# Feed-forward gate and up products as a 2x2 block product of seven parts, with tokens in two spans

## The chip, the cores and the metric

The program runs on one core of one Trainium2 chip, in one launch. The metric is the device time of that core in microseconds (us), as the median of several runs.

## The reference

One inference step of a decoder layer, for 1024 prompt tokens and 8 x 4 = 32 sample tokens, 1056 together, with a model width of 1024, all in float32:

```
x  = x + 0.5 * ffn1(rmsnorm(x, n_ffn1))
x  = x + mixer(rmsnorm(x, n_mix))          # attention and pooling, not touched by the change
x  = x + 0.5 * ffn2(rmsnorm(x, n_ffn2))
y  = rmsnorm(x, n_final)
ffn(h) = (silu(h @ w_gate) * (h @ w_up)) @ w_down     # w_gate, w_up: 1024 x 2816, w_down: 2816 x 1024
rmsnorm(x, g) = x * rsqrt(mean(x * x) + 1e-6) * g
```

## The kernel before

The residual `xT` lies transposed in SBUF, with the 1024 features as 8 tiles of 128 partitions and the 1056 tokens along the free dimension, in three chunks of 352 (`CH`). Every product of two float32 matrices is made of three matmuls: each operand is split into a high part, which is the value rounded to the type fp32r, and a low part, the value less its high part, and `product3` (lines 112 to 114) adds hi x hi, hi x lo and lo x hi into one PSUM bank.

`stage_ffn` is called twice. The 2816 hidden features are 22 tiles (`FT`), taken in 11 pairs by a loop on each engine; the first and the last pair are written out. For each tile the gate and up weights (2 x 8 x 128 x 128) are loaded into `gu_raw`, copied to `gu_hi` by ScalarE (line 458) and their low parts subtracted by VectorE (line 541). TensorE then makes, for each of three chunks, 24 matmuls of 352 columns for gate and 24 for up. VectorE multiplies gate by the tokens' inverse root (`norm.inv`, line 572), ScalarE takes Silu (line 464), VectorE multiplies by the inverse root again (574) and by up (578), and splits the result into `a_hi` (581) and `a_lo` (583). After two tiles the down product follows: 24 blocks (3 chunks x 8 feature tiles) of 6 matmuls, each added to `xT` by one VectorE operation (line 589). The down weights are split like the others (lines 481 and 609).

RMSNorm is late: the products take x times gain (`in_h_hi` and `in_h_lo`, in the second stage `f_h_hi` and `f_h_lo`, lines 157 and 195), and the inverse root, which is made meanwhile (lines 201 to 215), is applied behind the product. For the second feed-forward, chunks 0 and 1 of these halves and the inverse roots are made in the last part of `stage_out_project`. In the first, the next stage's halves are made in the last pair. At the end of the second, `FinishRows` turns the result into rows of 128 tokens on TensorE (line 269), normalizes them and stores them; rows 0 to 4 are turned within the last pair, the others behind it.

GpSimd has no arithmetic in the feed-forward loops. Its subtracts that rows below show belong to the compression stage (cs), where it shares the making of low parts with VectorE (lines 1041 and 1035 on GpSimd, 1160, 1176 to 1178 and 1184 on VectorE).

## Time and profile before

| | us |
|---|---|
| median of three runs | 2868.22 (2865.53 to 2868.45) |
| span of the profiled execution | 2868.9 |
| TensorE busy with matmuls | 2649.2 (92%) |
| VectorE busy | 1484.9 (52%) |
| ScalarE busy | 885.1 (31%) |
| GpSimd busy | 384.7 (13%) |
| mean granted clock of TensorE | 0.975 of full speed |

Busy time is the time in which an instruction of an engine ran; matmuls overlap, so the distance between the starts of two of them says how long each takes of the stream. The granted clock is a share of 2.4 GHz. The profiled execution lies 0.7 us above the median.

### The profile page before, as it was taken

What the parts mean: (1) busy time and instruction counts of PE and PEld (TensorE: products, weight loads), DVE (VectorE), ACT (ScalarE), POOL (GpSimd) and SP (SyncE); (2) the same over time, 40 slices, a digit from 0 to 9 for tenths busy, and PEclk for the clock granted to TensorE, in tenths of its full rate; (3) what the DMA queues carried; (4) which work ended last, traced back from release to release, by engine and by line L of the source; (5) the groups of instructions that cost most, each with busy time, mean ns of one, the idle gap of its engine ahead of it and who ended that gap; (6) DMA issues with size and microseconds to landing.
All of it is one profiled execution on the core that took longest, in us unless ns stands there. A gap on an engine that the chain in (4) does not pass through costs nothing. (4 is left out here: it accounts for less than half of the span.)

```text
span 2868.9 us, 44901 instructions
## 1 busy us (share of the span) xinstructions
PE 2649.2 (92%) x17616; PEld 2498.9 (87%) x17616; DVE 1484.9 (52%) x2887; ACT 885.1 (31%) x1570; POOL 384.7 (13%) x427
## 2 busy tenths in 40 slices
PE   4999998999999999999978888777999999999997
PEld 4888887999999999988966666556999999999997
DVE  5444445554444444464147768555464444444445
ACT  4656655111111111032246656444221111111112
POOL 4444441000000000000012222452000000000001
PEclk9999999999999999999979979899999999999999
DMA  4131313211111110021311010586031111111101
GB/s 180 64 125 64 125 56 119 74 46 58 55 47 44 44 44 29 15 100 43 101 62 45 24 44 34 185 279 226 16 88 45 45 55 46 44 44 44 51 15 61
DMA packets 171831, 206.88 MB, mean 72 GB/s; under 512 B 15342, under 2 KB 153455, under 8 KB 169002
## 3 DMA queue, kind: packets, MB, share of 16 engines
q1 hardware_dynamic: 161026, 144.91, 16.3%
q0 software_dynamic: 10672, 60.19, 5.7%
q8 instruction: 86, 1.41, 0.2%
q14 instruction: 47, 0.39, 0.0%
HBM read 191.39 MB, written 18.01 MB: 73 GB/s over the span
## 5 line engine op out<-in xcount | busy, mean ns | idle before, releaser
L464 ACT ACTIVATE f_act_gate<-f_act_gate 128x352 f32<-128x352 f32 x132 | 65.8, 498 | 1185.3 <-DVE f_act_gate L572 1185.2
L589 DVE SCALAR_TENSOR_TENSOR trunk<-f_down,trunk 128x352 f32<-128x352 f32 x528 | 275.9, 524 | 205.3 <-PE f_down L114 205.3
L112 PE MATMUL f_down<-f_a_hi,f_wd_hi 128*128 128x352 f32 x1056 | 341.1, 323 | 0.0
L114 PE MATMUL f_down<-f_a_hi,f_wd_lo 128*128 128x352 f32 x1056 | 340.3, 322 | 0.0
L113 PE MATMUL f_down<-f_a_lo,f_wd_hi 128*128 128x352 f32 x1056 | 339.3, 321 | 0.0
L112 PE MATMUL cs_sum<-cs_x_hi,cs_w_hi 128*128 128x256 f32 (+1 forms) x768 | 230.3, 300 | 33.0 <-DVE cs_x_lo L1184 21.6
L114 PE MATMUL cs_sum<-cs_x_hi,cs_w_lo 128*128 128x256 f32 (+1 forms) x768 | 218.0, 284 | 0.0
L113 PE MATMUL cs_sum<-cs_x_lo,cs_w_hi 128*128 128x256 f32 (+1 forms) x768 | 217.6, 283 | 0.0
L1041 POOL TENSOR_TENSOR cs_x_lo<-cs_x,cs_x_hi 128x516 fp32r<-128x516 f32 x128 | 170.9, 1335 | 235.4 <-ACT cs_x_hi L1098 235.4
L114 PEld LDWEIGHTS f_down<-f_a_hi,f_wd_lo 128*128 128x128 f32 x1056 | 199.1, 189 | 0.0
L113 PEld LDWEIGHTS f_down<-f_a_lo,f_wd_hi 128*128 128x128 f32 x1056 | 198.7, 188 | 0.1
L112 PEld LDWEIGHTS f_down<-f_a_hi,f_wd_hi 128*128 128x128 f32 x1056 | 198.1, 188 | 0.1
L578 DVE TENSOR_TENSOR f_act_up<-f_act_gate,f_up 128x352 f32<-128x352 f32 x132 | 68.8, 521 | 244.2 <-PE f_up L114 243.9
L112 PEld LDWEIGHTS cs_sum<-cs_x_hi,cs_w_hi 128*128 128x128 f32 x768 | 146.5, 191 | 44.1 <-DVE cs_x_lo L1184 41.9
L572 DVE TENSOR_TENSOR f_act_gate<-f_gate,f_inv 128x352 f32<-128x352 f32 x132 | 69.0, 523 | 214.5 <-PE f_gate L114 214.2
L112 PE MATMUL f_gate<-f_h_hi,f_gu_hi 128*128 128x352 f32 x528 | 170.1, 322 | 3.2 <-DVE f_gu_lo L557 3.2
L112 PE MATMUL f_gate<-in_h_hi,f_gu_hi 128*128 128x352 f32 x528 | 171.4, 325 | 0.0
L113 PE MATMUL f_gate<-in_h_lo,f_gu_hi 128*128 128x352 f32 x528 | 171.0, 324 | 0.0
L114 PE MATMUL f_gate<-in_h_hi,f_gu_lo 128*128 128x352 f32 x528 | 170.9, 324 | 0.0
L114 PE MATMUL f_up<-f_h_hi,f_gu_lo 128*128 128x352 f32 x528 | 170.5, 323 | 0.0
L114 PE MATMUL f_gate<-f_h_hi,f_gu_lo 128*128 128x352 f32 x528 | 170.5, 323 | 0.0
L113 PE MATMUL f_gate<-f_h_lo,f_gu_hi 128*128 128x352 f32 x528 | 170.3, 323 | 0.0
(421 smaller groups left out, 6745.6 us busy)
## 6 DMA issues: line engine op xcount, KB each, us to landing
f_gu_raw<-in_w_ffn_gate_dram SPq DMA_DIRECT2D x44, 512.0 KB, 4.3
f_gu_raw<-in_w_ffn_up_dram SPq DMA_DIRECT2D x44, 512.0 KB, 5.7
as_pages<-in_cache_kv_slc_dram SPq DMA_DIRECT2D x128, 128.0 KB, 4.0
as_pages<-in_cache_kv_slc_dram POOLq DMA_DIRECT2D x128, 128.0 KB, 4.0
at_spread<-saved_rows SPq DMA_DIRECT2D x16, 768.0 KB, 3.9
in_w_raw<-in_w_ffn_down_dram SPq DMA_DIRECT2D x11, 1024.0 KB, 5.0
f_wd_raw<-in_w_ffn_down_dram SPq DMA_DIRECT2D x11, 1024.0 KB, 5.0
x_saved<-trunk SPq DMA_DIRECT2D x2, 2112.0 KB, 14.8
```

Source lines behind the costliest of these rows:

```text
L112: pe.matmul(out, w_hi, x_hi, start=first, stop=False)
L113: pe.matmul(out, w_hi, x_lo, start=False, stop=False)
L114: return pe.matmul(out, w_lo, x_hi, start=False, stop=last)
L464: act.activation(act_gate[:, b, :], act_gate[:, b, :], ACT.Silu).then_inc(silu_done, 1)
L572: dve.tensor_tensor(act_gate[:, b, :], gate_bank[b][:, 0:CH], inv, ALU.mult).then_inc(gate_scaled, 1)
L578: dve.tensor_tensor(act_up[:], act_gate[:, b, :], up_bank[b][:, 0:CH], ALU.mult).then_inc(pair_free, 1)
L589: dve.scalar_tensor_tensor(xT[:, m, chunk(c)], down_bank[n % 4][:, 0:CH], 0.5, xT[:, m, chunk(c)], ALU.mult, ALU.add).then_inc(down_free, 1)
L1041: pool.tensor_tensor(x_lo[s][:, 0:ODD], x[s][:, 0:ODD], x_hi[s][:, 0:ODD].bitcast(F32), ALU.subtract).then_inc(diff_lo_done, 1)
```

## The change

Gate and up of one tile, over 2 x 264 tokens, are a 2x2 block product: the weights' halves (gate and up, each with features 0 to 511 and 512 to 1023) times the tokens' halves (features 0 to 511 and 512 to 1023, each for 264 tokens `near` and 264 tokens `far`). Eight block products and four additions become seven block products (Winograd's form), four sums of weight blocks (`w_sum`), four differences of token blocks (`b_sum`), and additions of the results. Each block product is 4 x 3 matmuls of 264 columns (`HT`).

- The tokens are taken in two spans of 528: all 22 tiles for the first span, then all 22, backwards, for the second. A step `g` is one tile for one span; 44 steps, in 22 pairs `q`, with a down product of 16 blocks of 6 matmuls behind each pair. The weights are loaded twice, but for the tile at which the order turns.
- GpSimd makes the four weight sums of the next tile, the low parts of two of the seven weight blocks (4 and 6) and one addition of results (`up_far`) in each step. VectorE makes the low parts of the other five, the other additions (`base`, `above`, `far`, `up_near`), and as before the multiplications, the splits and the updates. ScalarE makes the high parts and copies two products out of PSUM, whose banks are then added onto.
- Weight blocks have one buffer each: the high part of block i of the next tile is written when product i of this step is done.
- The inverse root is now multiplied into the operands, so that it is needed before the first product; operands are made once for each span, at the start and during pair 10, by VectorE (`scaled`, `difference`, `low_b`), ScalarE and GpSimd (`last_b`, `low_b`). `stage_out_project` no longer makes halves for the second feed-forward.
- In the second feed-forward rows 0 to 3 are finished in pairs 16 to 19 (`EARLY`), rows 4 and 5 are turned in the last pair, the others behind it.
- All loops over pairs are written out. The split token operands `b_hi` and `b_lo` lie in the buffers of the halves before; a new `b_sum` of 8 x 4 x 264 floats for each partition is added.

The core of the diff, without empty lines, and with less indentation:

```diff
+    STEPS, PAIRS, WEIGHTS = 2 * FT, FT, 2 * FT - 1
+    KH = KT // 2
+    ON_DVE, ON_POOL = (0, 1, 2, 3, 5), (4, 6)
+    SUM_OF = {1: 0, 2: 1, 3: 2, 5: 3}
+    PLACED = (0, 2, 3, 1, 0, 2, 3)
...
+    def sums(v):
+        raw = gu_raw[v % 2]
+        gate_1, gate_2, up_1, up_2 = raw[:, 0, 0:KH], raw[:, 0, KH:KT], raw[:, 1, 0:KH], raw[:, 1, KH:KT]
+        pool.wait_ge(raw_landed[v % 2], 32 * (v // 2) + 32)
+        if v:
+            pool.wait_ge(w_lo_dve, 5 * (v - 1) + 2)
+        pool.tensor_tensor(w_sum[:, 0], up_1, up_2, ALU.add).then_inc(w_summed, 1)
+        if v:
+            pool.wait_ge(w_lo_dve, 5 * (v - 1) + 3)
+        pool.tensor_tensor(w_sum[:, 1], gate_1, up_1, ALU.subtract).then_inc(w_summed, 1)
+        if v:
+            pool.wait_ge(w_lo_dve, 5 * (v - 1) + 4)
+        pool.wait_ge(w_summed, 4 * v + 1)
+        pool.tensor_tensor(w_sum[:, 2], w_sum[:, 0], gate_1, ALU.subtract).then_inc(w_summed, 1)
+    def last_sum(v):
+        if v:
+            pool.wait_ge(w_lo_dve, 5 * (v - 1) + 5)
+        pool.wait_ge(w_summed, 4 * v + 3)
+        pool.tensor_tensor(w_sum[:, 3], gu_raw[v % 2][:, 0, KH:KT], w_sum[:, 2],
+                           ALU.subtract).then_inc(w_summed, 1)
+    def low_w(v, i):
+        pool.wait_ge(w_hi_done, 7 * v + i + 1)
+        pool.tensor_tensor(w_lo[:, i], form(v, i), w_hi[:, i].bitcast(F32), ALU.subtract).then_inc(w_lo_pool, 1)
+    def last_b(span):
...
+        if span:
+            pool.wait_ge(product_done, 7 * FT)
+        pool.tensor_tensor(b_sum[:, 6], b_sum[:, 4], b_sum[:, 3], ALU.subtract).then_inc(b_last_made, 1)
+    def low_b(span, i):
+        pool.wait_ge(b_hi_done, 7 * span + {5: 4, 6: 7}[i])
+        pool.tensor_tensor(b_lo[:, i], b_sum[:, i], b_hi[:, i].bitcast(F32), ALU.subtract).then_inc(b_lo_pool, 1)
+    def operands(span):
+        last_b(span)
+        low_b(span, 5)
+        low_b(span, 6)
...
+    for g in range(STEPS):
+        v = next_weights(g)
+        pool.wait_ge(above_done, g + 1)
+        pool.wait_ge(fifth_copied, g + 1)
+        if g:
+            pool.wait_ge(far_done, g)
+        pool.tensor_tensor(up_far[:], above[:], fifth_copy[:], ALU.add).then_inc(up_far_done, 1)
+        if v is not None:
+            low_w(v, 4)
+            if v + 1 < WEIGHTS:
+                sums(v + 1)
+            low_w(v, 6)
+            if v + 1 < WEIGHTS:
+                last_sum(v + 1)
...
+    def high_w(v, i):
+        if i in SUM_OF:
+            act.wait_ge(w_summed, 4 * v + SUM_OF[i] + 1)
+        else:
+            act.wait_ge(raw_landed[v % 2], 32 * (v // 2) + 32)
+        if v:
+            before = v - 1 if v <= FT - 1 else v
+            act.wait_ge(product_done, 7 * before + i + 1)
+        act.activation(w_hi[:, i], form(v, i), ACT.Copy).then_inc(w_hi_done, 1)
...
+    def copy_out(g, target, bank, nth, copied_sem, free_sem):
+        act.wait_ge(product_done, 7 * g + nth + 1)
+        if g:
+            act.wait_ge(free_sem, g)
+        act.activation(target[:], bank_set[g % 2][bank][:, 0:HT], ACT.Copy).then_inc(copied_sem, 1)
...
+    for q in range(PAIRS):
+        fresh = q == 0 or down_of(q) != down_of(q - 1)
+        for g in (2 * q, 2 * q + 1):
+            v = next_weights(g)
+            copy_out(g, first_copy, 0, 0, first_copied, base_done)
+            if v is not None:
+                high_w(v, 0)
+            copy_out(g, fifth_copy, 2, 1, fifth_copied, up_far_done)
+            if v is not None:
...
+                norm.square(act, xT, 2)
+            if fresh and g == 2 * q and q:
+                high_down(down_of(q), 0)
+            if v is not None:
+                high_w(v, 2)
+                high_w(v, 3)
+            if fresh and g == 2 * q and q:
+                high_down(down_of(q), 1)
+            act.wait_ge(product_done, 7 * g + 5)
+            if g:
+                act.wait_ge(a_near, g)
+            act.activation(near[:], bank_set[g % 2][0][:, 0:HT], ACT.Silu).then_inc(silu_near, 1)
+            if v is not None:
+                high_w(v, 4)
+            if g == 1:
+                act.wait_ge(norm.sum_done, 6)
+                for s in range(2):
+                    high_down(0, s)
...
+            if g == 1:
                 norm.root(act, 2)
-        act.wait_ge(wd_landed, 16 * i + 16)
-        act.wait_ge(down_done, DOWNS * i + ONE)
-        act.activation(wd_hi[:], wd_raw[:], ACT.Copy).then_inc(wd_hi_done, 1)
-        if not last:
...
+    def scaled(span, k0, first, step):
+        part = slice(2 * span * HT, 2 * span * HT + 2 * HT)
+        for k in range(KH):
+            made = dve.scalar_tensor_tensor(
+                b_sum[:, first:first + step + 1:step, k, :],
+                xT[:, k0 + k, part].rearrange("p (h n) -> p h n", h=2), norm.gain[:, k0 + k:k0 + k + 1],
+                inv[:, part].rearrange("p (h n) -> p h n", h=2), ALU.mult, ALU.mult)
+        made.then_inc(b_made, 1)
...
+    def difference(out, a, b):
+        dve.tensor_tensor(b_sum[:, out], b_sum[:, a], b_sum[:, b], ALU.subtract).then_inc(b_made, 1)
+    def low_b(span, i):
+        dve.wait_ge(b_hi_done, 7 * span + {0: 1, 1: 2, 4: 3, 2: 5, 3: 6}[i])
+        dve.tensor_tensor(b_lo[:, i], b_sum[:, i], b_hi[:, i].bitcast(F32), ALU.subtract).then_inc(b_lo_dve, 1)
...
+    def left_operands(span):
+        if span:
+            dve.wait_ge(product_done, 7 * (FT - 1) + 1)
+        scaled(span, 0, 0, 7)
+        dve.wait_ge(b_made, 5 * span + 1)
...
+        dve.wait_ge(b_made, 5 * span + 2)
+        low_b(span, 0)
+    def right_operands(span):
+        if span:
+            dve.wait_ge(product_done, 7 * (FT - 1) + 6)
+        scaled(span, KH, 4, 1)
+        dve.wait_ge(b_made, 5 * span + 3)
+    def middle_operands(span):
+        difference(2, 5, 7)
+        difference(3, 5, 1)
+        dve.wait_ge(b_made, 5 * span + 5)
...
+    def multiply(g, h, gate, up, gate_ready, up_ready, done, hi_done, ready):
+        s = tile_of(g) % 2
+        dve.wait_ge(gate_ready, g + 1)
+        dve.wait_ge(up_ready, g + 1)
+        dve.tensor_tensor(gate[:], gate[:], up[:], ALU.mult).then_inc(done, 1)
+        dve.wait_ge(done, g + 1)
+        dve.tensor_copy(a_hi[:, s, h], gate[:]).then_inc(hi_done, 1)
+        dve.wait_ge(hi_done, g + 1)
+        dve.tensor_tensor(a_lo[:, s, h], gate[:], a_hi[:, s, h].bitcast(F32), ALU.subtract).then_inc(ready, 1)
...
+    def update(q, n):
+        h, m = order_of(q)[n // KT], n % KT
+        span = 0 if q < FT // 2 else 1
+        dve.wait_ge(down_done, DOWNS * q + n + 1)
+        dve.scalar_tensor_tensor(xT[:, m, half_of(span, h)], bank_set[0][n % 4][:, 0:HT], 0.5,
+                                 xT[:, m, half_of(span, h)], ALU.mult, ALU.add).then_inc(down_free, 1)
...
+    for q in range(PAIRS):
+        fresh = q == 0 or down_of(q) != down_of(q - 1)
+        for g in (2 * q, 2 * q + 1):
+            v = next_weights(g)
+            banks = bank_set[g % 2]
+            if v is not None:
+                low_w(v, 0)
+                low_w(v, 1)
...
+            if fresh and g == 2 * q and q:
+                low_down(down_of(q), 0)
+            if v is not None:
+                low_w(v, 2)
+            dve.wait_ge(product_done, 7 * g + 4)
+            dve.wait_ge(first_copied, g + 1)
+            if g:
+                dve.wait_ge(up_near_done, g)
+            dve.tensor_tensor(base[:], first_copy[:], banks[1][:, 0:HT], ALU.add).then_inc(base_done, 1)
+            dve.wait_ge(base_done, g + 1)
+            if g:
+                dve.wait_ge(up_far_done, g)
+            dve.tensor_tensor(above[:], base[:], banks[3][:, 0:HT], ALU.add).then_inc(above_done, 1)
+            if v is not None:
+                low_w(v, 3)
+            if fresh and g == 2 * q and q:
+                low_down(down_of(q), 1)
+            dve.wait_ge(product_done, 7 * g + 6)
+            if g:
+                dve.wait_ge(a_far, g)
+            dve.tensor_tensor(far[:], base[:], banks[2][:, 0:HT], ALU.add).then_inc(gate_far_done, 1)
+            if g == 1:
+                for s in range(2):
+                    low_down(0, s)
+            multiply(g, 1, far, up_far, silu_far, up_far_done, far_done, a_hi_far, a_far)
...
+            dve.tensor_tensor(up_near[:], base[:], banks[3][:, 0:HT], ALU.add).then_inc(up_near_done, 1)
+            multiply(g, 0, near, up_near, silu_near, up_near_done, near_done, a_hi_near, a_near)
+            if v is not None:
+                low_w(v, 5)
+            if g == 0:
+                norm.fold(dve, 2)
+            if g == 1:
...
+    def product(g, i):
+        span, first, in_set = g // FT, g % FT == 0, g % 2
+        v = weights_of(g)
+        if i in ON_DVE:
+            pe.wait_ge(w_lo_dve, 5 * v + ON_DVE.index(i) + 1)
+        else:
+            pe.wait_ge(w_lo_pool, 2 * v + ON_POOL.index(i) + 1)
+        if first and i < 5:
+            pe.wait_ge(b_lo_dve, 5 * span + i + 1)
+        elif first:
+            pe.wait_ge(b_lo_pool, 2 * span + i - 4)
+        if i < 4 and in_set == 0 and g:
+            pe.wait_ge(down_free, DOWNS * (g // 2 - 1) + 13 + PLACED[i])
...
+        elif i < 4 and g > 1:
+            pe.wait_ge((silu_near, base_done, gate_far_done, up_near_done)[PLACED[i]], g - 1)
+        elif i >= 4:
+            pe.wait_ge({4: first_copied, 5: fifth_copied, 6: above_done}[i], g + 1)
+        if finish and in_set and i == 0 and g // 2 - 1 in EARLY:
+            fin.wait_taken(pe, EARLY[g // 2 - 1])
...
+            mm = product3(pe, out, w_hi[:, i, k, :], w_lo[:, i, k, :], b_hi[:, i, k, :], b_lo[:, i, k, :],
+                          k == 0 and i < 4, k == KH - 1, i >= 4)
+        mm.then_inc(product_done, 1)
...
+    def down_part(q, n, part):
+        h, m = order_of(q)[n // KT], n % KT
+        s = tile_of(2 * q + part) % 2
+        if n % KT < 4:
+            pe.wait_ge((a_near, a_far)[h], 2 * q + part + 1)
+        if part == 0:
+            if n >= 4:
+                pe.wait_ge(down_free, DOWNS * q + n - 3)
+            else:
+                pe.wait_ge((silu_near, base_done, gate_far_done, up_near_done)[n], 2 * q + 1)
+        return product3(pe, bank_set[0][n % 4][:, 0:HT], wd_hi[:, s, m * P:(m + 1) * P],
+                        wd_lo[:, s, m * P:(m + 1) * P], a_hi[:, s, h], a_lo[:, s, h], part == 0, part == 1)
...
+    for q in range(PAIRS):
+        for g in (2 * q, 2 * q + 1):
+            for i in range(7):
+                product(g, i)
...
+                    norm.total(pe, bank_set[0][3], 2)
+        pe.wait_ge(wd_split, down_of(q) + 1)
+        if q == 0:
+            pe.wait_ge(norm.var_done, CHUNKS)
+        for n in range(4):
+            down_part(q, n, 0)
+        for n in range(4):
+            down_part(q, n, 1).then_inc(down_done, 1)
+        for n in range(4, DOWNS):
+            down_part(q, n, 0)
...
-        norm.high(act, xT, mix_hi, c)
...
-        dve.wait_ge(done, KT)
-        norm.low(dve, xT, mix_hi, mix_lo, 0, range(m, m + 1))
...
-        if m < 4:
-            dve.wait_ge(done, 2 * KT)
-            norm.low(dve, xT, mix_hi, mix_lo, 1, range(2 * m, 2 * m + 2))
```

The form of a block is a piece of `gu_raw` for 0, 4 and 6, and of `w_sum` for 1, 2, 3 and 5. Behind both steps of a pair VectorE runs the 16 updates, in the order n = 0 to 15.

## Rows read from the trace of the kernel before

**Rows 1.** Busy time of the engines in stretches, granted clock (PEclk), DMA share, GB/s.

```profile
core 0: us, PE busy (x) PEld busy (x) DVE busy (x) ACT busy (x) POOL busy (x), PEclk, DMA share, GB/s
471.60:1231.00 759.40, 755.71 (x4712) 754.95 (x4712) 389.89 (x660) 113.69 (x130) 4.55 (x9) 1.00 0.16 49
2080.00:2849.00 769.00, 766.59 (x4796) 765.40 (x4796) 384.55 (x664) 111.89 (x128) 3.85 (x3) 1.00 0.16 46
1640.00:1710.00 70.00, 55.40 (x280) 41.63 (x280) 43.48 (x95) 36.95 (x119) 21.72 (x25) 0.78 0.12 46
```

**Rows 2.** TensorE's waits in the two feed-forward stretches: total, times, longest.

```profile
PE f_down L181 <- DVE f_sq L172: 3.7, 1, 3.7
...
PE f_gate L112 <- DVE f_gu_lo L557: 3.2, 1, 3.2
```

**Rows 3.** Matmuls in order of time (start, length), first and last of 18 and 15.

```profile
1227.75 0.32 PE L112 MATMUL f_down<-f_a_hi,f_wd_hi 128*128 128x352 f32 x1
...
1230.47 0.32 PE L114 MATMUL f_down<-f_a_hi,f_wd_lo 128*128 128x352 f32 x1
...
394.14 0.28 PE L112 MATMUL cs_sum<-cs_x_hi,cs_w_hi 128*128 128x256 f32 x1
...
395.80 0.28 PE L114 MATMUL cs_sum<-cs_x_hi,cs_w_lo 128*128 128x256 f32 x1
```

**Rows 4.** VectorE (DVE) and GpSimd (POOL) in order of time, compression stage.

```profile
32.46 0.68 DVE L1160 TENSOR_TENSOR cs_w_lo<-cs_w_whole,cs_w_hi 128x512 fp32r<-128x512 f32 x1
...
33.17 1.74 POOL L1041 TENSOR_TENSOR cs_x_lo<-cs_x,cs_x_hi 128x516 fp32r<-128x516 f32 x1 [1.64 <-ACT cs_x_hi L1098]
...
33.67 1.79 DVE L1160 TENSOR_TENSOR cs_w_lo<-cs_w_whole,cs_w_hi 128x512 fp32r<-128x512 f32 x1
...
34.87 1.73 POOL L1035 TENSOR_TENSOR cs_w_whole<-cs_w_whole 128x512 f32<-128x512 f32 x1
35.38 1.25 DVE L1176 COPY cs_x<-cs_pe 128x2 f32<-128x2 f32 x1
```

**Rows 5.** Groups of VectorE: line, names, shapes, count, busy us, mean ns, idle before.

```profile
L581 DVE CAST f_a_hi<-f_act_up 128x352 fp32r<-128x352 f32 x132 | 45.4, 344 | 4.5
...
L169 DVE TENSOR_TENSOR f_sq<-f_sq 128x1408 f32<-128x1408 f32 x2 | 3.2, 1617 | 0.0
...
L172 DVE TENSOR_TENSOR op_w_raw<-op_w_raw 128x704 f32<-128x704 f32 x2 | 1.8, 892 | 0.1
```

**Rows 6.** The same view for ScalarE (ACT).

```profile
L1091 ACT ACTIVATE cs_x<-cs_turn 128x256 f32<-128x256 f32 x128 | 48.0, 375 | 35.9 <-PE cs_turn L1273 35.9
...
L1070 ACT ACTIVATE cs_w_hi<-cs_w_whole 128x512 fp32r<-128x512 f32 x12 | 6.6, 616 | 0.0
...
L468 ACT ACTIVATE f_gu_hi<-f_gu_raw 128x1024 fp32r<-128x1024 f32 x2 | 2.0, 1048 | 11.0 <-PEq L2745 11.0
```

**Rows 7.** The same view for GpSimd.

```profile
L1885 POOL TENSOR_TENSOR trunk<-at_scaled,at_upper 64x256 f32<-64x256 f32 x32 | 23.1, 723 | 2.5
...
L1880 POOL TENSOR_TENSOR at_scaled<-at_scaled 128x512 f32<-128x512 f32 x16 | 20.4, 1272 | 20.9 <-DVE at_scaled L2004 20.6
```

**Rows 8.** Again VectorE and GpSimd in order of time, compression stage.

```profile
335.02 1.31 POOL L1041 TENSOR_TENSOR cs_x_lo<-cs_x,cs_x_hi 128x516 fp32r<-128x516 f32 x1 [2.52 <-ACT cs_x_hi L1098]
...
335.34 0.42 DVE L1177 TENSOR_TENSOR cs_x<-cs_turn,cs_x 128x256 f32<-128x256 f32 x1 [0.96 <-ACT cs_x L1091]
...
336.01 0.60 DVE L1184 TENSOR_TENSOR cs_x_lo<-cs_x,cs_x_hi 128x256 fp32r<-128x256 f32 x1
```

**Rows 9.** Loads: destination and source, count, KB each, median us to landing.

```profile
f_gu_raw<-in_w_ffn_up_dram SPq DMA_DIRECT2D x44, 512.0 KB, 5.7
```

**Rows 10.** VectorE in order of time at the start of the first feed-forward.

```profile
466.08 0.52 DVE L201 TENSOR_SCALAR f_var<-f_down 128x352 f32<-128x352 f32 x1 [2.06 <-PE f_down L187]
...
475.62 2.34 DVE L207 RECIPROCAL f_inv<-f_inv 128x352 f32<-128x352 f32 x1
```

**Rows 11.** Gate matmuls of both stages: ns min/median/max, first and last start in us.

```profile
L112 PE MATMUL f_gate<-in_h_hi,f_gu_hi x528: 320/323/807, 471.6 to 1211.0; 128*128 128x352 f32 x176
...
L112 PE MATMUL f_gate<-f_h_hi,f_gu_hi x528: 318/323/592, 2080.4 to 2815.8; 128*128 128x352 f32 x176
```

More of the change, by code:

```diff
@@ new lines, in stage_ffn @@
+        a_lo = mem.sb(scope, name + "_a_lo", [P, 2, 2, HT], F32R)
+        first_copy, fifth_copy, base, above, up_far, up_near, far, near = [
+            mem.sb(scope, f"{name}_{part}", [P, HT])
+            for part in ("first", "fifth", "base", "above", "up_far", "up_near", "far", "near")]
+        doubles = [mem.ps(scope, f"{name}_bank{i}", (P, 2 * BANK)) for i in range(4)]
+        singles = [x[:, i * BANK:(i + 1) * BANK] for x in doubles for i in range(2)]
+        bank_set = [singles[0:4], singles[4:8]]
@@ new lines, in high_down @@
+                def high_down(w, s):
+                    act.wait_ge(wd_landed, 16 * w + 16)
+                    q = w if w < FT // 2 else w + 1
+                    if q:
+                        act.wait_ge(down_done, DOWNS * q)
+                    act.activation(wd_hi[:, s], wd_raw[:, s], ACT.Copy).then_inc(wd_hi_done, 1)
+                for c in range(0 if prepared else 2):
+                    norm.square(act, xT, c)
+                if not prepared:
+                    norm.root(act, 0)
```

596 lines of the change are left out of this document (289 added, 307 removed).

## The prediction

> **What bounds the kernel now.** I read the busy tenths first: TensorE is at 9 in every slice of the two feed-forward stages (about 471 to 1231 us, and 2080 to 2849 us), then the stretches themselves [rows 1]. There TensorE is busy 755.7 of 759.4 us and 766.6 of 769.0 us at the full granted clock (1.00, its 2.4 GHz level), VectorE about half, ScalarE a seventh, GpSimd almost not at all. The lists of waits have 3.7 us for TensorE at the beginning of the first and 3.2 at the beginning of the second as their largest rows [rows 2]. So both stages are a gapless stream of matmuls, and their length is count times slot. Slots come from starts in order of time [rows 3]: 18 matmuls of 352 columns start from 1227.75 to 1230.47, so 2.72/17 = 0.160 us each; 15 of 256 columns start from 394.14 to 395.80, 1.66/14 = 0.1185. One feed-forward is 3168 gate and up matmuls (22 tiles x 3 chunks x 2 x 8 x 3) and 1584 down matmuls, 4752 x 0.1597 = 759 us, which the stretch confirms.
>
> **TensorE after the change.** A product is 4 x 3 matmuls of 264 columns. Between the two measured sizes a slot is 0.1185 + (8/96) x 0.0415 = 0.122. One step (one tile, one span) is 84 matmuls, 10.2 us; two steps and their down part (96 matmuls, 11.7 us), a pair, are 264 x 0.1215 = 32.1 us, and a feed-forward has 22 pairs. The old kernel takes 759/22 = 34.5 us for the same work. TensorE alone would win 2.4 us a pair, 44 x 2.4 = 106 us in all. The question is what the other engines do to the 32.1.
>
> **Their new work, per step.** VectorE: five low halves of 512 elements (0.68 long, next start 0.60 later [rows 4]), four adds of a PSUM bank, twice multiply, cast, subtract. An element costs it 1.03 ns (1408 against 704 elements: (1617 - 892)/704 [rows 5]), so a 264-element operation is 0.43 to 0.44 (892 - 440 x 1.03 ns); a cast is 0.34 at 352 [rows 5], about 0.28 here. In the even step of a pair come two low halves of the down weights, 1024 elements, 1.22 each by the same rate. After the steps come 16 updates of 0.43. Sum for a pair: 10 x 0.68 + 8 adds and 8 multiply/subtracts x 0.43 + 4 casts x 0.28 + 2 x 1.22 + 16 x 0.43 = 24.1 us. ScalarE: seven copies of 512 (0.62), two of 264 (0.38), two Silu (taken as 0.42), and in the even step 2 x 1.05 [rows 6]: 6 to 8 us of a 10.2 us step. GpSimd, idle before: six operations of 512 at 1.27 and one of 264 (0.74, between 0.72 at 256 and 1.27 at 512) [rows 7]: 8.4 us a step, 16.7 a pair.
>
> No engine has more than 32.1 us of work. If that were all, the only gap would be before the fifth down block, 0.6 us, since VectorE comes to its updates 0.6 us late: a pair of 32.8.
>
> **The row that decides.** Rows 4 show VectorE and GpSimd together. VectorE starts three subtracts of two SBUF inputs, of 0.68 us alone; GpSimd's subtract is issued at 33.17, under the second. It lasts to 34.91 (1.74 rather than 1.27: it began when the second VectorE operation ended). VectorE's third, issued at 33.67, lasts 1.79: it ended 0.55 after GpSimd's. GpSimd's next, issued at 34.87, lasts 1.73, and under it a two-element copy of VectorE takes 1.25. One operation of each, in turn, and each waits for the whole of the other. At 335 to 337 us [rows 8] two VectorE operations with one input in PSUM run at 0.41 to 0.42 under a GpSimd operation, and the third, with both inputs in SBUF, takes 0.60 and ends 0.28 after it. So what collides is: two SBUF inputs or an SBUF to SBUF copy on VectorE, against GpSimd's two-input operations.
>
> This is a rule of the Trainium skill, SBUF — State Buffer, section Who interferes with whom: VectorE and GpSimd share one port pair that is locked for a whole instruction, and a VectorE instruction with two SBUF inputs, or a copy in a 2-port mode, contends with a GpSimd instruction that reads SBUF. The trace agrees, 1.79 against 0.68 us. By this rule a pair comes to 42.0 below; without it, to 32.8.
>
> In the new loops a pair holds this resource 16.7 us for GpSimd and, on VectorE, for 10 low halves, 2 down halves, 8 multiply/subtracts and 4 casts, some 11 to 14 us: 28 to 31 of 32.1. That alone would just fit. But both engines run in written order, and VectorE's order is a chain that TensorE waits for.
>
> **Walk through a pair** (us from TensorE's first product; a product's result is visible 0.2 after its slots). Even step: VectorE is alone until *above* is made at 7.85, because GpSimd's loop begins by waiting for *above*; product 6, due at 8.76, needs it and starts in time. From then on both have work. GpSimd: up_far to 9.1, low 4 10.2 to 11.45, three sums and low 6 to 17.6. VectorE: second down half 9.1 to 10.2, far add 10.6, Silu on ScalarE to 11.1, and then multiply, cast, subtract, multiply, cast each behind one GpSimd operation: the step ends with low 5 at 18.9, where it would be 13.9 alone. Odd step (TensorE from 10.2): product 5 needs that low 5 and starts at 19.1, not 17.5 (1.6 late). Then low 0, GpSimd's last sum (1.25), low 1, low 2, base, above: 22.75; product 6 starts at 22.9 and ends at 24.4, where the even flow would be 20.4 (another 2.3 to 2.4). The first four down halves end at 25.9; the rest needs a_far: low 3, far add, Silu 24.25, multiply behind low 4 (25.65), cast behind sum 0 (27.1), subtract behind sum 1: 28.65. TensorE waits 2.9. Next, near multiply and cast, behind sum 2 and low 6, its subtract, and low 5 end at 32.65, and only then come the updates: the fifth down block, ready at 30.2, starts at 33.2, 3.0 late. Twelve blocks of 0.73 later the pair ends at 42.0. Stalls 1.6 + 2.3 + 2.9 + 3.0 = 9.8. Nothing is carried over: at 42.6 VectorE and GpSimd are drained, so the next pair is the same. Raw weights are not late: the load waits for low 6 (17.6), lands 5.7 us later [rows 9], and the sum that reads it starts at 25.6.
>
> Bounds of a pair: 37 if half of the blocked operations slip through between GpSimd's, 45 if semaphore steps cost 0.1 more at each of some 30 links. I take the walk, as every link in it has a row: 42.0. Feed-forward loops: 44 x (42.0 - 34.5) = **+330**.
>
> **Beginnings.** Stage one now needs both inverse roots before a product. On VectorE: mean square (466.6 [rows 10]), low 0 (470.5), invert 4.5 (reciprocal 2.34 and four small ones, 0.52 like the mean square or less [rows 10]), mean square, five lows, invert again: 482.5; four scalings of 528 elements (2.8), difference and low of 1056 (1.2 each): product 0 at 487.8. Right operands 2.8, middle 2.4, four lows of 1.2, with three 2.4 us operations of GpSimd in turn between them: the first step ends at 509, as if it had begun at 499. Before, the first gate matmul was at 471.6 [rows 11] with 3.7 us of wait behind it: **+24** (16 without collisions). Stage two has its roots, but the same operands to make: scaling from 2078, last product near 2110, as if begun at 2100, against 2080.4 [rows 11] and 3.2 of wait [rows 2]: +16, less 3 for the halves no longer made in the output projection, whose TensorE hardly waited for them: **+13**. The change of span in pair 10 adds VectorE 5.2 us before base, 2.8 before the updates, 7 among them, and 7 on GpSimd, less one step without weights: 8 each, **+16**. The last rows: four go early, about 2 us of VectorE each, and five turns leave the last pair, **+2** (from -5 to +8). Moved waits on SP's queue: its loads have slack, 0. Unrolled loops: 0, as cs matmuls that are written out one by one keep 0.1185 [rows 3].
>
> The granted clock falls to 0.78 in a stretch where TensorE is fed in pieces [rows 1]; a pair's 17 us of pieces at that level would cost 7.3/0.78 - 7.3 = 2.1, most of it under waits. I take 0 and keep 44 x 2 = 88 as the far end.
>
> Sum: 330 + 24 + 13 + 16 + 2 = 385. The profiled span is 2868.9, 0.7 over the median of the runs, so 2868.2 + 385 = **3253 us**, own range 3160 to 3350.
>
> **Rivals.**
> *Half the collisions* (0.18): GpSimd and VectorE fall into a phase in which the short casts and adds slip past. Pair 37.5: 44 x 3.0 + 45 = 3045. For it: VectorE's holds are shorter than its durations (0.55 of 0.68). Against: rows 4 and 8 show no operation that slipped.
> *TensorE still bounds* (0.10), the other side: the waits are covered, pair 32.8, 44 x -1.7 = -75, beginnings and seam without collisions 16 + 8 + 10 + 2: 2829. It decides from the point where a pair stays under 34.5 - 36/44 = 33.7, that is where collisions cost TensorE less than 0.9 a pair. For it: no engine is over its 32.1. Against it: five blocked operations in the even step alone.
> *Slow clock as well* (0.10): pieces of 1.5 us with gaps of 2 to 3 us hold TensorE at its 1.2 GHz level past the stall, pair 44 to 45: 3253 + 88 to 130, about 3360.
> *The forecast* (0.60). The rest (0.02): about no change.
>
> **Numbers.** Predicted 3253. The range must reach towards the half-collision case and the clock case: 3020 to 3350 leaves out the TensorE case, most of the clock case and little else. 0.2% (6 us) is what a measurement can tell. Faster 0.10, same 0.02, slower 0.88.
>
> **What would show it.** Right: TensorE busy about 0.75 to 0.8 in the new loops, waits of matmuls on a_lo, above, w_lo and trunk of 2 to 3 us each per pair; low halves of 512 on VectorE with a mean well above 0.68 and some at 1.8; GpSimd 512 operations above 1.27; slots of 0.122; first product near 488. Wrong: TensorE at 0.98 and VectorE subtracts at 0.68 while GpSimd works, or stalls that sit on loads or on ScalarE. The prediction fails if GpSimd's operations fall in time where VectorE does updates, which have a PSUM input.

## The result, and the profile after

| | before | after |
|---|---|---|
| median, us | 2867.93 (2865.53 to 2868.45) | 3208.74 (3204.67 to 3215.08, four runs) |
| span of the profiled execution | 2868.9 | 3209.6 |
| mean granted clock | 0.975 | 0.936 |

The ratio is 1.1189, 95% interval [1.1167, 1.1212]: 341 us slower, where 385 were forecast; 3208.7 lies inside the range of 3020 to 3350.

By stretches of the two traces: the first feed-forward, from 471.6 us to the end of its last update (1241.2 before, 1420.8 after), grew from 769.6 to 949.2 (+179.6). What lies between the two became 3.6 shorter. The second, from the last update of the output projection to its own last update, grew from 773.0 to 941.7 (+168.8), and the end became 4.0 shorter. Together that is +341, the difference of the two spans.

The page of the kernel after: busy time of the engines, then their tenths in 40 slices, which for TensorE (PE) were 9 in these stages before.

```profile
PE 2666.7 (83%) x19728; PEld 2478.3 (77%) x19728; DVE 2192.5 (68%) x3746; ACT 1258.6 (39%) x2397; POOL 1280.2 (40%) x1043
...
PE   5999976888888888889988888779588888888887
```

Stretches, with columns as in [rows 1]: the whole first stage, the whole second, one pair of 40.2 us, 3 us behind a stall in it, and eight pairs in a row.

```profile
471.60:1420.80 949.20, 778.28 (x5816) 755.66 (x5816) 754.09 (x1113) 305.57 (x556) 447.70 (x313) 0.92 0.25 74
2253.30:3195.30 942.00, 779.05 (x5860) 757.64 (x5860) 754.19 (x1120) 317.02 (x569) 452.93 (x313) 0.93 0.25 74
703.00:743.20 40.20, 34.35 (x264) 33.44 (x264) 32.34 (x49) 12.71 (x24) 19.94 (x15) 0.96 0.28 79
706.00:709.00 3.00, 2.11 (x10) 1.80 (x9) 2.93 (x5) 0.00 (x0) 1.70 (x3) 0.60 0.02 6
603.90:931.26 327.36, 278.61 (x2114) 271.32 (x2113) 258.45 (x385) 101.71 (x193) 159.21 (x113) 0.94 0.27 78
```

VectorE (DVE) is busy less than TensorE in the pair, and TensorE 34.35 of 40.2 us, so neither is full. [Rows 1] had 755.71 of 759.40. What TensorE waits for, as in [rows 2]:

```profile
PE f_bank L113 <- DVE f_above L806: 93.7, 42, 5.5
PE f_bank L113 <- DVE f_a_lo L756: 80.1, 40, 2.2
PE f_bank L113 <- DVE trunk L762: 70.1, 48, 2.4
...
PE f_bank L113 <- DVE f_w_lo L689: 31.4, 39, 13.1
```

In every pair these are three waits of 1 to 2 us, on `above`, on `a_lo` and on the updates (`trunk`), and a short one on a low part of the weights. All are waits for VectorE; none of a size is for loads or ScalarE. VectorE's odd step in order of time (start, length), as in [rows 4]:

```profile
699.17 0.43 DVE L806 TENSOR_TENSOR f_above<-f_base,f_bank 128x264 f32<-128x264 f32 x1
...
701.03 1.32 DVE L752 TENSOR_TENSOR f_far<-f_far,f_up_far 128x264 f32<-128x264 f32 x1 [0.49 <-ACT f_far L643]
702.38 1.25 DVE L754 CAST f_a_hi<-f_far 128x264 fp32r<-128x264 f32 x1
703.67 1.37 DVE L756 TENSOR_TENSOR f_a_lo<-f_far,f_a_hi 128x264 fp32r<-128x264 f32 x1
704.97 0.42 DVE L822 TENSOR_TENSOR f_up_near<-f_base,f_bank 128x264 f32<-128x264 f32 x1
705.49 0.98 DVE L752 TENSOR_TENSOR f_near<-f_near,f_up_near 128x264 f32<-128x264 f32 x1
706.50 1.26 DVE L754 CAST f_a_hi<-f_near 128x264 fp32r<-128x264 f32 x1
707.80 0.43 DVE L756 TENSOR_TENSOR f_a_lo<-f_near,f_a_hi 128x264 fp32r<-128x264 f32 x1
708.15 0.68 DVE L689 TENSOR_TENSOR f_w_lo<-f_w_sum,f_w_hi 128x512 fp32r<-128x512 f32 x1
708.75 1.95 DVE L762 SCALAR_TENSOR_TENSOR trunk<-f_bank,trunk 128x264 f32<-128x264 f32 x5
```

GpSimd in the same 9 us:

```profile
699.67 1.14 POOL L502 TENSOR_TENSOR f_up_far<-f_above,f_fifth 128x264 f32<-128x264 f32 x1 [2.03 <-DVE f_above L806]
700.77 1.29 POOL L472 TENSOR_TENSOR f_w_lo<-f_gu_raw,f_w_hi 128x512 fp32r<-128x512 f32 x1
702.02 1.46 POOL L454 TENSOR_TENSOR f_w_sum<-f_gu_raw 128x512 f32<-128x512 f32 x1
703.44 1.31 POOL L457 TENSOR_TENSOR f_w_sum<-f_gu_raw 128x512 f32<-128x512 f32 x1
704.72 1.46 POOL L461 TENSOR_TENSOR f_w_sum<-f_w_sum,f_gu_raw 128x512 f32<-128x512 f32 x1
706.14 1.47 POOL L472 TENSOR_TENSOR f_w_lo<-f_gu_raw,f_w_hi 128x512 fp32r<-128x512 f32 x1
```

And TensorE's waits in this step, the matmul that ended each and, in brackets, its length and who ended it:

```profile
699.74 0.36 PE L113 MATMUL f_bank<-in_h_hi,f_w_hi 128*128 128x264 f32 x1 [2.06 <-DVE f_above L806]
705.10 0.59 PE L113 MATMUL f_bank<-f_a_hi,f_wd_hi 128*128 128x264 f32 x1 [2.21 <-DVE f_a_lo L756]
709.23 0.39 PE L113 MATMUL f_bank<-f_a_hi,f_wd_hi 128*128 128x264 f32 x1 [1.12 <-DVE trunk L762]
```

From these rows: the ends of VectorE's multiply (702.35), cast (703.63) and subtract (705.04) lie 0.29, 0.15 and 0.29 us behind the end of a GpSimd operation (702.06, 703.48, 704.75). The addition at 704.97, with an input in PSUM, takes its 0.42. From 707.61 on GpSimd has nothing to do, and the next subtract takes 0.43. Three groups by line over both stages follow, with their means. Undisturbed, this subtract takes 0.43 us, the cast 0.30 and GpSimd's addition 0.74:

```profile
L756 DVE TENSOR_TENSOR f_a_lo<-f_far,f_a_hi 128x264 fp32r<-128x264 f32 x88 | 114.8, 1305 | 3.0
...
L754 DVE CAST f_a_hi<-f_far 128x264 fp32r<-128x264 f32 x88 | 103.6, 1177 | 3.0
...
L502 POOL TENSOR_TENSOR f_up_far<-f_above,f_fifth 128x264 f32<-128x264 f32 x88 | 98.5, 1119 | 718.6 <-DVE f_above L806 718.6
```

### The profile page after: what moved, and what is told of

The parts are those of the page before. It is cut to its first block and busy times, and to the rows that moved or that the text cites. A ratio compares the mean times of both kernels' runs of the same rounds, so it can differ in the third digit from the quotient of the medians.

```text
span 3209.6 us, 52342 instructions
## 1 busy us (share of the span) xinstructions
PE 2666.7 (83%) x19728; PEld 2478.3 (77%) x19728; DVE 2192.5 (68%) x3746; ACT 1258.6 (39%) x2397; POOL 1280.2 (40%) x1043
## 5 line engine op out<-in xcount | busy, mean ns | idle before, releaser
L113 PE MATMUL f_bank<-f_a_hi,f_wd_hi 128*128 128x264 f32 x1408 | 444.3, 316 | 159.1 <-DVE f_a_lo L756 80.1
L114 PE MATMUL f_bank<-f_a_lo,f_wd_hi 128*128 128x264 f32 x1408 | 432.8, 307 | 0.0
L115 PE MATMUL f_bank<-f_a_hi,f_wd_lo 128*128 128x264 f32 x1408 | 432.1, 307 | 0.0
L113 PE MATMUL f_bank<-in_h_hi,f_w_hi 128*128 128x264 f32 x1232 | 357.8, 290 | 82.8 <-DVE f_above L806 48.7
L113 PE MATMUL f_bank<-f_h_hi,f_w_hi 128*128 128x264 f32 x1232 | 358.8, 291 | 79.6 <-DVE f_above L806 45.0
L115 PE MATMUL f_bank<-f_h_hi,f_w_lo 128*128 128x264 f32 x1232 | 353.8, 287 | 0.0
L114 PE MATMUL f_bank<-f_h_lo,f_w_hi 128*128 128x264 f32 x1232 | 353.7, 287 | 0.0
L115 PE MATMUL f_bank<-in_h_hi,f_w_lo 128*128 128x264 f32 x1232 | 352.8, 286 | 0.0
L114 PE MATMUL f_bank<-in_h_lo,f_w_hi 128*128 128x264 f32 x1232 | 352.3, 286 | 0.0
L591 ACT ACTIVATE f_first<-f_bank 128x264 f32<-128x264 f32 x88 | 34.3, 390 | 679.1 <-PE f_bank L115 677.5
L115 PEld LDWEIGHTS f_bank<-f_a_hi,f_wd_lo 128*128 128x128 f32 x1408 | 298.3, 212 | 0.0
L472 POOL TENSOR_TENSOR f_w_lo<-f_gu_raw,f_w_hi 128x512 fp32r<-128x512 f32 x172 | 274.2, 1594 | 17.7 <-ACT f_w_hi L578 17.7
```

What stands on the lines that cost most here:

```text
L113: pe.matmul(out, w_hi, x_hi, start=first, stop=False, skip_group_check=onto)
L114: pe.matmul(out, w_hi, x_lo, start=False, stop=False, skip_group_check=onto)
L115: return pe.matmul(out, w_lo, x_hi, start=False, stop=last, skip_group_check=onto)
L472: pool.tensor_tensor(w_lo[:, i], form(v, i), w_hi[:, i].bitcast(F32), ALU.subtract).then_inc(w_lo_pool, 1)
L591: act.activation(target[:], bank_set[g % 2][bank][:, 0:HT], ACT.Copy).then_inc(copied_sem, 1)
```

## The experiments

All are edits of the kernel after. The pair is the time from one `up_far` to the second one behind it, which is one pair of steps; waits are TensorE's. The kernel after has pairs of 40.2 and 41.7 us in turn, mean 40.9. The first four ran beside a before of 2872.20 (2868.65 to 2874.03), the next four beside 2868.78 (2865.24 to 2871.30).

**1. Weight sums only once** (the sums of later tiles are left out, so TensorE works with those of the first; all else is done).

```diff
-    pool.tensor_tensor(w_sum[:, 0], up_1, up_2, ALU.add).then_inc(w_summed, 1)
+    if v:
+        pool.sem_inc(w_summed, 1)
+    else:
+        pool.tensor_tensor(w_sum[:, 0], up_1, up_2, ALU.add).then_inc(w_summed, 1)
```

> The changed kernel with the four weight sums made for the first tile only; later they are left out (the semaphores still count), so the results are not the reference's. Changed kernel: 3209 us, 40.9 us a pair. Collision theory (VectorE operations with two SBUF inputs and its casts wait for the whole of a GpSimd operation): four of GpSimd's seven operations a step are gone, five or six blocked turns in a pair of about 1 us go with them, pair 35 to 36, 2950 to 3000 us, and the cast's mean on VectorE falls from 1.2 towards 0.3 us. Order theory (VectorE's own list is too long, GpSimd only happens to run beside it): no change, 3200 us. Supplier theory (TensorE waits for what GpSimd makes): at most 1 us a pair, 3165 us, since no wait of TensorE names GpSimd.

Measured 2907.33 (2907.07 to 2907.60), ratio 1.0124 [1.0095, 1.0154], clock 0.964. The pair is a constant 33.54. In the loop the waits on `above` and `a_lo` are gone (4.5 and 4.2 us are left of them in all); the one left is on the updates, 1.3 a pair:

```profile
PE f_bank L113 <- DVE trunk L774: 58.5, 48, 1.6
```

VectorE has the same list as in the kernel after, and 88% of the loss is gone. So it isn't VectorE's own work that makes the pair long, but GpSimd's sums beside it. This run alone doesn't tell whether they do so by what they read or by being in the way on GpSimd.

**2. GpSimd's list later in the odd step.**

```diff
     if v is not None:
+        if g % 2:
+            pool.wait_ge(a_near, g + 1)
         low_w(v, 4)
```

> The changed kernel with one more wait on GpSimd: in the second step of a pair it begins low parts and sums only when VectorE has made a_near, so that it works while VectorE does the updates, which have one input in PSUM. Same work on every engine. Collision theory: a_far is ready 3 us earlier, the updates begin 3 to 4 us earlier, pair 36, 2990 us (2960 to 3040). Order theory: no change, 3209. Supplier theory: GpSimd's results come later, so slower than 3209 or equal.

Measured 3040.09 (3038.09 to 3042.08), ratio 1.0587 [1.0556, 1.0617]. The pair is 36.3. The operations are the same, nearly half of GpSimd's at another time, and 169 us are gone. In the odd step the casts take 0.30, in the even one still 1.27. The wait on `a_lo` is gone, that on the updates falls to 22.1, that on `above` stays at 93.5 us: it belongs to the odd step's beginning, behind the even step's collisions. The pair came as forecast (36), but 2990 took its gain for all 44 pairs. At the beginnings and turns there is none: in the first stage those pairs last 49.94 and 46.60 us, as against 49.56 and 46.57 in the kernel after.

**3. The two casts on ScalarE.**

```diff
-    dve.tensor_copy(a_hi[:, s, h], gate[:]).then_inc(hi_done, 1)
...
     act.activation(far[:], far[:], ACT.Silu).then_inc(silu_far, 1)
+    act.wait_ge(far_done, g + 1)
+    act.activation(a_hi[:, tile_of(g) % 2, 1], far[:], ACT.Copy).then_inc(a_hi_far, 1)
```

> The changed kernel with the four casts of a pair (a_hi) moved from VectorE to ScalarE. Collision theory: each cast costs a turn of 1.25 us behind GpSimd although it takes 0.28 alone; 1 us each minus 0.3 for the way to ScalarE and back: pair 37.5 to 38.5, 3060 to 3105 us. Order theory: 4 x 0.28 us shorter a pair at best, 3160 us; with the way to ScalarE no gain.

Measured 3195.63 (3193.09 to 3198.18), ratio 1.1128 [1.1096, 1.1161]: a miss, 13 us instead of 100 to 150. The pair is 40.4. VectorE has four casts of 1.2 us less in a pair, but two things take their place. It stands idle for 0.56 us at each cast, until ScalarE has made it. And collisions go to what follows: the near chain now ends before GpSimd's list does, and the low part behind it pays. In the odd step both cost about the same, 1.1 us each.

```profile
702.98 1.74 DVE L693 TENSOR_TENSOR f_w_lo<-f_w_sum,f_w_hi 128x512 fp32r<-128x512 f32 x1
```

The mean of the low parts rises from 827 to 1071 ns, and the wait on the updates from 70.1 to 128.6 us. So as long as GpSimd's list goes on, taking an operation away from VectorE can move a collision to the next one. What this run would have given without the way over ScalarE, it doesn't show.

**4. All on VectorE.** Its list gets GpSimd's seven operations of each step.

```diff
+    dve.tensor_tensor(up_far[:], above[:], fifth_copy[:], ALU.add).then_inc(up_far_done, 1)
...
+    pool_low(v, 4)
     low_w(v, 5)
+    pool_low(v, 6)
+    if v + 1 < WEIGHTS:
+        all_sums(v + 1)
```

> The changed kernel with GpSimd's seven operations of every step on VectorE, nothing left for GpSimd in the loops. VectorE gets 7.9 us more of work a pair (24.1 to 32). Collision theory: it runs without waits for GpSimd, updates begin about 29 us after the first product, pair 38 to 39, 3090 to 3130 us: faster than sharing. Order theory: the list that is too long gets 7.9 us longer, pair 46 to 49, 3430 to 3560 us.

Measured 3194.06 (3192.34 to 3195.78), ratio 1.1123 [1.1091, 1.1155]. VectorE's operations have their undisturbed durations, and the pair is 40.1, where 38 to 39 was expected. So GpSimd's help is worth next to nothing in this order: with it or without it the pair is the same within 1 us. The expected gain of 80 to 120 was 15: VectorE now is busy with the sums when updates are due (waits on them 173.9 us, up to 4.3 each), and the clock takes its part, below.

**5. GpSimd busy, but only writing** (each later sum is left out and replaced by three fills of 512 elements; its low parts still read).

```diff
+MEMSETS = 3
...
-    pool.tensor_tensor(w_sum[:, 0], up_1, up_2, ALU.add).then_inc(w_summed, 1)
+    if v:
+        for _ in range(MEMSETS - 1):
+            filled.wait(pool)
+            filled.did(pool.memset(w_sum[:, 0], 0.01))
+        filled.wait(pool)
+        pool.memset(w_sum[:, 0], 0.01).then_inc(w_summed, 1)
```

> The kernel after the change, but each of the four weight sums, from the second tile on, is replaced by three fills of 512 elements with a constant on GpSimd. So GpSimd stays busy between its low parts, but only writes SBUF. What is left out: the seven-product form gets constants for its sums, so the result is not the reference's. Theory of a shared read path: VectorE's operations with two SBUF inputs aren't held up by a fill, so the pair is near that of the run without sums, 33.5 to 35 us, and the whole 2905 to 2970 us. Rival, GpSimd being busy at all (or its place in the order) is what costs: pair near 41, whole near 3200 us. In between (casts held up, subtracts not): pair 36 to 38.

Measured 2914.41 (2914.24 to 2914.57), ratio 1.0160 [1.0131, 1.0190]. The pair is 33.7, as without sums. GpSimd in order of time, in an even step:

```profile
726.72 1.14 POOL L460 MEMSET f_w_sum<- 128x512 f32 x2
...
728.39 1.15 POOL L470 MEMSET f_w_sum<- 128x512 f32 x2
```

VectorE under these fills:

```profile
727.10 0.30 DVE L785 CAST f_a_hi<-f_far 128x264 fp32r<-128x264 f32 x1
727.44 0.43 DVE L787 TENSOR_TENSOR f_a_lo<-f_far,f_a_hi 128x264 fp32r<-128x264 f32 x1
...
728.78 0.30 DVE L785 CAST f_a_hi<-f_near 128x264 fp32r<-128x264 f32 x1
```

Casts and subtracts run at 0.30 and 0.43 under GpSimd's writes, and at 1.25 and 1.37 under its reads. In the odd step most fills ran beside the updates, as they waited for weights, so the even step is the evidence; over both stages the 117 such subtracts that begin under a fill take 0.43 to 0.44. The Trainium skill, SBUF — State Buffer, section Who interferes with whom, states that a VectorE instruction with two SBUF inputs contends with a GpSimd instruction that reads SBUF and not with one that only writes it; the trace agrees, 0.43 us under a fill.

**6 and 7. A dose of GpSimd work, at two places.** In the first feed-forward alone GpSimd multiplies 512 elements of a scratch buffer by themselves: once in each of 42 steps ahead of its sums (6), or twice in each of 20 pairs behind the first update (7).

```diff
     low_w(v, 4)
+    if not prepared:
+        one_more()                      # 6
...
+    if g % 2 and not prepared:
+        pool.wait_ge(down_free, DOWNS * (g // 2) + 1)
+        one_more()                      # 7
+        one_more()
```

> The kernel after the change, with one more GpSimd multiply of 512 elements in each step of the first feed-forward, ahead of the weight sums, on a scratch buffer nobody reads. If GpSimd's operations count by the turns they take from VectorE's chain, each costs about its own length: 1.3 us a step, 22 pairs x 2.6 = up to 57 us, whole 3240 to 3270 us. If the pair is set by something else than GpSimd's list (supply of weights, the clock, VectorE's own length), it costs under 10 us: 3209 to 3219. The second feed-forward is untouched and shows the same pair as before.

> The same two more GpSimd multiplies of 512 elements a pair in the first feed-forward, but behind the first of VectorE's 16 updates, which have an input in PSUM. By the theory of collisions of two-input SBUF operations this costs nothing, 3205 to 3215 us, although GpSimd has as much more to do as in the run with the dose in the chain. If what counts is how much GpSimd has to do, it costs the same as there, about 3240 to 3270.

Measured: 6, 3267.89 (3264.06 to 3271.71), ratio 1.1393 [1.1350, 1.1435], 59 us over the kernel after; 7, 3209.26 (3208.08 to 3210.44), ratio 1.1188 [1.1156, 1.1221], 0.5 over it. The pair of the first stage is 43.7 in the one and 40.8 in the other. That is 59/42 = 1.4 us for each operation of 1.2: in the chain it costs its full length and a bit, among VectorE's updates it costs nothing that can be measured. The bit is the clock: in eight pairs of 6 (606.88 to 956.79 us) the waits are 1.77 us a pair longer than in the kernel after, TensorE's busy time 1.05, and the granted clock is 0.90. In 7, the row of GpSimd's extra work:

```profile
708.27 2.16 POOL L456 TENSOR_TENSOR f_more<-f_more 128x512 f32<-128x512 f32 x2
```

And an update that starts beside it, at its full speed:

```profile
709.09 0.43 DVE L776 SCALAR_TENSOR_TENSOR trunk<-f_bank,trunk 128x264 f32<-128x264 f32 x1 [0.76 <-PE f_bank L115]
```

**8. The same work in another order.** GpSimd's low parts and sums begin behind the near subtract, in both steps of nearly all pairs; in the odd step ScalarE makes weight blocks 1 to 6 behind the far Silu, and VectorE the low parts of 1, 2, 3 and 5 among the updates.

```diff
+    WEIGHED_BEHIND = {3: 1, 5: 2, 8: 3, 11: 5}
+    def moved(g):
+        return 2 <= g and g // 2 not in (FT // 2 - 1, PAIRS - 1)
...
+    if moved(g) and g % 2 == 0:
+        pool.wait_ge(a_near, g + 1)
+        low_w(v, 4)
+        low_w(v, 6)
+        if v + 1 < WEIGHTS:
+            first_sums(v + 1)
+    elif moved(g):
+        pool.wait_ge(a_near, g + 1)
+        if moved(g - 1):
+            third_sum(v)
+            last_sum(v)
+        low_w(v, 4)
+        low_w(v, 6)
...
     update(q, n)
+    if moved(2 * q + 1) and n in WEIGHED_BEHIND:
+        low_w(next_weights(2 * q + 1), WEIGHED_BEHIND[n])
```

> Nothing left out, only another order of the same operations: GpSimd makes its low parts and sums behind the near multiply's subtract of a step (so beside TensorE's stream and VectorE's updates), and in the odd step ScalarE and VectorE make the weight blocks 1 to 6 behind the far Silu and among the updates. By the theory of collisions most of the stalls go: pair 34 to 35.5 us, whole 2900 to 2990 us. If the length of the engines' own lists bounds the pair, it stays near 40 and the whole near 3150 to 3200. A new risk is that the weights of the next step, made later, are late for products 1 to 5 of the next even step: then waits of TensorE on w_lo of some us a pair, and a whole of 3000 to 3100.

Measured 2899.81 (2897.88 to 2901.73), ratio 1.0109 [1.0079, 1.0139], clock 0.962. The pair is 32.60 through both stages, but 34.3 where rows are finished in it: better than the 34 to 35.5 expected, under the 34.5 of the kernel before, and nearly TensorE's own 32.3. The first stretch is 14.5 pairs of the first stage, the one where the order turns (46.6 us) among them, at a granted clock of 0.99; the second is eight pairs without a turn:

```profile
604.19:1095.62 491.43, 476.22 (x3864) 472.02 (x3863) 383.35 (x715) 187.09 (x350) 287.27 (x203) 0.99 0.31 92
592.34:853.14 260.80, 258.39 (x2114) 256.71 (x2113) 201.15 (x385) 100.88 (x193) 156.23 (x112) 1.00 0.37 109
```

TensorE's longest waits in that stage; the first row is its beginning, the third step 0 and the turn:

```profile
PE f_bank L113 <- DVE in_h_lo L734: 23.0, 4, 17.7
PE f_bank L113 <- DVE trunk L791: 10.8, 23, 1.2
PE f_bank L113 <- DVE f_above L837: 9.7, 2, 5.5
```

Most of VectorE's blocked time is gone: in eight pairs it is busy 201.15 us instead of 258.45 (198.77 without the sums, experiment 1), and over both stages its casts have a mean of 342 ns instead of 1154 to 1177. What is left of the collisions has moved to other operations, as two groups of low parts show, one of VectorE and one of GpSimd:

```profile
L718 DVE TENSOR_TENSOR f_w_lo<-f_gu_raw,f_w_hi 128x512 fp32r<-128x512 f32 x86 | 112.0, 1303 | 74.4 <-ACT f_w_hi L606 74.3
...
L484 POOL TENSOR_TENSOR f_w_lo<-f_gu_raw,f_w_hi 128x512 fp32r<-128x512 f32 x172 | 293.0, 1721 | 196.7 <-DVE f_a_lo L785 186.0 <-ACT f_w_hi L606 10.7
```

Their means were 738 and 1594 ns in the kernel after. TensorE hardly waits for these.

**9. The beginnings of 8 in another order.** At the start the first inversion goes ahead of the first low part and, in step 0, base and above ahead of low parts 1 and 2; the norm's third sum comes after product 5 and its mean square ahead of the near chain. In the second stage GpSimd's first sums wait until VectorE has made its first scalings and difference, and in the pairs at the turn and at the end GpSimd's list starts behind the near subtract.

```diff
+    if prepared:
+        pool.wait_ge(b_made, 2)
     sums(0)
...
+    norm.invert(dve, 0)
     low_w(0, 0)
-    norm.invert(dve, 0)
...
-    if g == 1 and i == 3:
+    if g == 1 and i == 5:
```

> The reordered kernel with its beginnings put in another order as well, nothing left out. At the start of the first stage the first inversion goes ahead of the first low part (VectorE sits idle 3.2 us there); base and above of the first step go ahead of low parts 1 and 2 (TensorE waits 4.2 us); the norm's column sums for the third chunk come after product 5 instead of 3 (waits of 3.7 and 5.2 us in the two stages) and its mean square ahead of the near chain (2.8 us each); in the second stage GpSimd's first sums wait for VectorE's first difference, so that they don't collide with the scalings (about 4 us); in pair 10 and the last pair GpSimd's list starts behind the near subtract (1 to 3 us each). If each of these stalls is its own: 25 to 30 us less than the reordered kernel, 2868 to 2878 us, as much as the kernel before. Rival: VectorE's list is gapless in the beginnings (476 to 512 us, 2093 to 2131 us), so that what is taken from one wait comes back in the next, and only the removed idle and collisions count: 8 to 12 us less, 2888 to 2892.

Measured 2891.22 (2886.27 to 2895.70, six runs), ratio to a before of 2872.02 (2862.25 to 2874.36) 1.0072 [1.0056, 1.0089]: the rival's figure. The first product of the second stage starts 6.4 us sooner (1.3 of it had been won ahead of the stage), and the second waits longer, 11.40 us where it was 6.38, as the sums now meet VectorE's second four scalings, which take 6.87 us where they were 2.80:

```profile
2099.09 6.87 DVE L729 SCALAR_TENSOR_TENSOR f_b_sum<-trunk,f_gain,f_inv 128x528 f32<-128x528 f32 x4
...
2099.22 0.59 PE L113 MATMUL f_bank<-f_h_hi,f_w_hi 128*128 128x264 f32 x1 [7.99 <-DVE f_w_lo L724]
2113.63 0.56 PE L113 MATMUL f_bank<-f_h_hi,f_w_hi 128*128 128x264 f32 x1 [11.40 <-DVE f_h_lo L740]
```

No version here beats the kernel before. In 8 the loops gain 44 x 1.9 = 84 us, and it still is 31 us slower, so the rest takes some 115. From product 0 to product 0 its first pairs last 61.5 and 66.1 us in the two stages and the pairs at the turns 47.2, where others last 32.6; the first product of the first stage comes 18 us later than before, and the row-finishing pairs take 1.6 more each. The token sums can't simply be made earlier, since `b_sum`, which the list of the change calls new, lies in the memory of the operands' low parts in use; whether another place for it would help, no run shows.

## Why the prediction was right, point by point

**The mechanism** stands. Sums taken out (1), only writes in their place (5), the same reads behind the near subtract and beside the updates (8): each time the pair goes to 32.6 to 33.7. One more read put into the chain costs 1.4 us (6), and put beside the updates nothing (7). The prediction's pair without collisions, 32.8, is near what 8 shows, 32.60, with 0.30 of wait at the fifth down block where 0.6 was said.

**The pair, 42.0, was 40.9**, but its terms were not right, and that they nearly cancel is luck. The table has eight pairs of the first stage in each kernel, the third to the tenth: for each pair its length, the time for which TensorE waits and is busy, and the granted clock.

| | stretch, us | pair | waits | busy | clock |
|---|---|---|---|---|---|
| after | 603.90 to 931.26 | 40.92 | 6.09 | 34.83 | 0.94 |
| 4, all on VectorE | 607.15 to 927.93 | 40.10 | 5.49 | 34.61 | 0.93 |
| 3, casts on ScalarE | 601.38 to 924.68 | 40.41 | 5.82 | 34.59 | 0.95 |
| 2, odd step late | 598.52 to 888.71 | 36.27 | 2.70 | 33.58 | 0.97 |
| 1, no sums | 584.01 to 852.31 | 33.54 | 1.26 | 32.27 | 1.00 |
| 8, reordered | 592.34 to 853.14 | 32.60 | 0.30 | 32.30 | 1.00 |

*The waits* were forecast as 1.6, 2.3, 2.9 and 3.0, together 9.8. In these pairs of the kernel after they are 0.41, 2.06, 2.20 and 1.41. The walk has VectorE's turns in the right order, but is a little long: from `above` to the last low part of the step it has 11.05 us in the even step and 9.9 in the odd one, and the trace 10.3 and 9.2. The last wait is shorter for another reason too, the clock. In the odd step shown above the twelve matmuls between the wait on `a_lo` and that on the updates start 0.22 us apart and take 3.0 us (705.10 to 708.11), where the walk has 1.5, so TensorE comes to the updates later and waits less:

```profile
705.49 0.42 PE L114 MATMUL f_bank<-f_a_lo,f_wd_hi 128*128 128x264 f32 x1
705.71 0.42 PE L115 MATMUL f_bank<-f_a_hi,f_wd_lo 128*128 128x264 f32 x1
```

*The granted clock*, the term that was set to 0, made up for a good part of it. The granted clock of 706 to 709 us, right behind the stall, is 0.60, so TensorE runs most of it at its 1.2 GHz level. The 264 matmuls of a pair keep it busy for 34.83 us, and for 32.30 in 8 at a granted clock of 1.00: 2.5 us a pair. The prediction had named 2 a pair as the far end and said that most of it would lie under waits; some does, as shown, and shortens the last wait. In this account the clock was mis-sized by 44 x 2.5 = +110 us, the waits by 44 x (6.1 - 9.8) = -163, and TensorE's own time by 44 x 0.2 = +9 (32.1 against 32.3), together -44, of the 44 x (40.9 - 42.0) = -48 by which the loops were too dear. The forecast of 3253 is nearer than its terms.

**The slot**: 0.122 was right, as a pair of 8 has 264 matmuls and 0.30 of waits in 32.60, and (32.60 - 0.30)/264 = 0.1223. The sum of the pair took 0.1215, which is where the 0.2 us come from. The loops not written as loops cost nothing that shows.

**The beginnings** were too cheap. The first product was due at 487.8 and started at 488.9. But beyond 22 pairs and its turn the first stage grew by 179.6 - 22 x 6.4 - 6.0 = 33 us instead of 24: products 1 to 4 waited 0.4 to 3.5 each, product 6 waited 4.2, the norm's sum 3.7, the first down block 5.5, and the granted clock from 470 to 530 is 0.72. The second grew by 168.8 - 22 x 6.4 - 6.0 = 22, where 16 and 2 for the last rows were said. Its first product waited 13.1 us, since GpSimd's first sums and VectorE's scalings meet (four scalings take 5.8 instead of 2.8), as VectorE in order of time shows:

```profile
2253.96 5.83 DVE L694 SCALAR_TENSOR_TENSOR f_b_sum<-trunk,f_gain,f_inv 128x528 f32<-128x528 f32 x4 [0.32 <-PEq L2977]
```

In each stage the two pairs where the order turns came to about 6.0 over two others, where 8 was said. In the middle 3.6 us were won that were forecast as 3, and at the end 4.0. With the loops at 44 x 6.4 = 282, where 330 was said, the sum is 282 + 33 + 22 + 12 - 4 - 4 = 341.

**The rivals.** Half the collisions (3045) didn't come true by itself, but experiment 2, in which those of the odd step are taken away on purpose, gave 3040. TensorE as the bound (2829) didn't happen: its condition, under 33.7 a pair, is met by 8 and 1, but they are at 2900 and 2907 and not at 2829, since that case had beginnings, turns and last rows at 36 us in all, and in 8 they cost some 115. The slow clock came true as a mechanism and in its size a pair (2 to 3 us); the shorter waits kept the time from 3360.

**The signs** that were to show it were met but for two: TensorE is busy 0.82 of the first stage, not 0.75 to 0.8, and the wait on a low part of the weights is 0.4 a pair, not 2 to 3.

What stays open: why pairs of 40.2 and 41.7 us alternate. Two in a row (603.90 to 644.05, and on to 685.65) have granted clocks of 0.96 and 0.92 with the same instructions, and no run here tells cause from effect.
